# The last projection as seven half-size products instead of eight, with x's sums moved to GpSimd

## The reference, cut to what matters

```python
def conv_ffn(hn, w_up, conv_w, conv_b, w_down):
    u = causal_dwconv(hn @ w_up.astype(hn.dtype), conv_w) + conv_b.astype(hn.dtype)
    a, b = jnp.split(u, 2, axis=-1)
    return (jax.nn.silu(a) * b) @ w_down.astype(hn.dtype)

h = h + conv_ffn(rmsnorm(h, norm2[layer]), ...)   # w_down: 2816 x 1024
h = rmsnorm(h, norm_f)
return h[:, N_META:]
```

## Time and profile before

| What | us |
|---|---|
| runs (median; lowest to highest) | 2037.92; 2035.79 to 2041.82 |
| the profiled execution's own time | 2038.91 |
| its span | 2037.1 |
| PE busy | 1983.4 (97%) |
| DVE busy | 1220.9 (60%) |
| ACT busy | 770.8 (38%) |
| GpSimd busy | 287.2 (14%) |
| DMA queue, share of 16 engines | 43.0% |

### The profile page before, as it was taken

How to read it: one execution, slowest core, us unless ns; L and a number is a source line. 1 busy time by engine, 2 the same in 40 slices (tenths; PEclk the granted TensorE clock), 3 DMA queues, 4 the chain that set the end, 5 groups by cost and what they waited for, 6 DMA issues and landing times.

```text
span 2037.1 us, 31749 instructions
## 1 busy us (share of the span) xinstructions
PE 1983.4 (97%) x13268; PEld 1902.2 (93%) x13268; DVE 1220.9 (60%) x1476; ACT 770.8 (38%) x1022; POOL 287.2 (14%) x276
## 2 busy tenths in 40 slices
PE   8999999999999999999999999997999999999998
PEld 8999998999999999899999999997999999988886
DVE  6457674666577555666533343389888787743533
ACT  5213333534333444434343333244444444332322
POOL 0000003659280122222000001100000000000101
PEclk9999999999999999999999999998999999999999
DMA  9235567664456664555342223311222221274442
GB/s 285 87 108 130 147 164 194 194 197 156 149 148 161 159 180 148 149 156 169 92 183 99 83 91 88 100 60 56 84 73 84 73 90 67 85 282 139 142 144 108
DMA packets 271619, 270.21 MB, mean 133 GB/s; under 512 B 147772, under 2 KB 215716, under 8 KB 271348
## 3 DMA queue, kind: packets, MB, share of 16 engines
q1 hardware_dynamic: 271476, 268.17, 43.0%
HBM read 188.55 MB, written 79.57 MB: 132 GB/s over the span
## 4 chain that ended last, share of the span: by engine, by line
PE 87%; DVE 6%; issue 2%; DMA 2%; ACT 2%; SPq 2%; DVEq 0%; ACTq 0%
PE a_psum L1046 32%; PE a_psum L1349 18%; PE a_psum L1358 12%; PE a_psum L154 10%; PE a_psum L1033 5%; PE a_psum L1121 1%; PE a_psum L1140 1%; PE a_psum L1225 1%; PE a_psum L1150 1%; PE a_psum L1103 1%; PE a_psum L1118 1%; PE a_psum L1166 1%; DMA w_raw<-in_w_in 1%; DVE ext L2097 1%; PE a_psum L1240 1%
## 5 line engine op out<-in xcount | busy, mean ns | idle before, releaser
L1046 PE MATMUL a_psum<-xh,w_hi 128*128 128x342 f32 (+3 forms) x1656 | 536.2, 324 | 1.4 <-DVE w_lo L1789 1.3
L1046 PE MATMUL a_psum<-xl,w_hi 128*128 128x342 f32 (+3 forms) x1656 | 531.9, 321 | 0.0
L1046 PE MATMUL a_psum<-xh,w_lo 128*128 128x342 f32 (+3 forms) x1656 | 530.0, 320 | 0.0
L1046 PEld LDWEIGHTS a_psum<-xh,w_hi 128*128 128x128 f32 x1656 | 312.7, 189 | 4.2 <-DVE w_lo L1789 1.9
L1046 PEld LDWEIGHTS a_psum<-xl,w_hi 128*128 128x128 f32 x1656 | 312.8, 189 | 1.0
L1046 PEld LDWEIGHTS a_psum<-xh,w_lo 128*128 128x128 f32 x1656 | 312.6, 189 | 0.0
L1493 ACT ACTIVATE post<-a_psum 128x342 f32<-128x342 f32 (+3 forms) x207 | 94.4, 456 | 553.3 <-PE a_psum L1046 516.5
L1789 DVE TENSOR_TENSOR w_lo<-w_raw,w_hi 128x1024 fp32r<-128x1024 f32 x87 | 110.2, 1267 | 153.6 <-ACT w_hi L1418 153.6
L1358 PE MATMUL a_psum<-act_hi,down_hi 128*128 128x512 f32 x352 | 139.7, 397 | 3.4 <-DVE act_lo L2298 3.4
L1358 PE MATMUL a_psum<-act_hi,down_lo 128*128 128x512 f32 x352 | 139.7, 397 | 0.0
L1358 PE MATMUL a_psum<-act_lo,down_hi 128*128 128x512 f32 x352 | 139.2, 396 | 0.0
(11 more groups left out here) (272 smaller groups left out, 3921.2 us busy)
## 6 DMA issues: line engine op xcount, KB each, us to landing
w_raw<-in_w_in SPq DMA_DIRECT2D x76, 512.0 KB, 3.8
down_raw<-in_w_ffn_down SPq DMA_DIRECT2D x44, 512.0 KB, 3.6
up_raw<-in_w_up SPq DMA_DIRECT2D x19, 1024.0 KB, 4.9
mix_scratch<-post SPq DMA_DIRECT2D x32, 522.0 KB, 2.8
act_scratch<-post SPq DMA_DIRECT2D x22, 512.0 KB, 2.6
act_raw<-act_scratch SPq DMA_DIRECT2D x44, 256.0 KB, 3.9
ext<-mix_scratch SPq DMA_DIRECT2D x9, 1024.0 KB, 7.0
y<-mix_scratch SPq DMA_DIRECT2D x18, 512.0 KB, 5.8
```

The lines of the kernel that those rows point to most:

```text
L1046: mm = pe.matmul(psum[:, u % 2, 0:n], w[:, k, :], x[:, k, at0:at0 + n], start=(k == 0 and part == 0), stop=(k == KC - 1 and part == 2))
```

## The change

1. The down projection becomes a 2x2 block product made of seven products: 11 k-tiles of 128 (KH) against 4 tiles of 128 output channels and 512 tokens, 77 steps of 4 x 3 matmuls. Each step loads a 128x512 weight tile and a 128x512 activation tile. With p the product, operands are blocks of w_down and of the activation, or sums of blocks.
2. The sums of w_down (`ws`, four) are made in DRAM by eight transfers on GpSimd's own queue: four copies at input tile 5, two accumulating transfers at tile 12, and one each at tiles 77 and 80. Each is 1408 x 512 floats.
3. The sums of the activation (`ts`, four) are made by GpSimd as each block's product is done (`act_sums`): one 128x512 instruction for j under 11, three for j from 11 on; SP stores them (`store_sums`), and for j from 11 on first loads the partner block's half and sum (`load_sums`). ACT's first taps wait for these.
4. The results of the seven products are added on DVE (`down_add`, eight instructions of 128x2048, and eight of 128x256 at the end), with one ACT copy out of PSUM (128x2048).
5. Eight weight slots instead of six; three steps are prepared ahead of the seam (DEARLY) where it was one, the fourth between the last block's taps, and the rest behind `store_sums(21)` on SP. The ACT table for Ln and Exp is loaded at the seam, not at the end.
6. The last four steps run in two chunks of 256 tokens; the norm runs over three column ranges, with 24 output transfers.
7. At the change of form, x's four sums, the first pair's four quarter sums and the split of x block 5 go from DVE to GpSimd; the first pair's products come in the order 0, 2, 3, 1, 4, 5, 6; one `x_low` waits for the last sum.

```diff
-NDOWN = 2 * FT
-DW, DA, DIN = 6, 8, 3
+KH = FT // 2
+NDOWN = 7 * KH
+DW, DA, DIN, DEARLY = 8, 8, 3, 3
...
+            def load_sums(j):
+                k = j - KH
+                sp.wait_ge(act_st[k % 2], 16 * (k // 2 + 1))
+                sp.wait_ge(sum_st, sums_stored(j - 1))
+                sp.dma_start(ts_one[:, :], sc["act"][k][:, 512:1024]).then_inc(sum_in, 16)
+                sp.dma_start(ts_two[:, :], sc["ts"][0, k]).then_inc(sum_in, 16)
+            def store_sums(j):
+                for n, (kind, x) in enumerate(((0, ts_one),) if j < KH else
+                                              ((2, ts_one), (1, ts_two), (3, acc_of(j, 1)[:, 0:512]))):
+                    sp.wait_ge(p_q, summed_act(j) if j < KH else summed_act(j - 1) + n + 1)
+                    sp.dma_start(sc["ts"][kind, j % KH], x[:, 0:512]).then_inc(sum_st, 16)
...
+                store_act(j - 1)
+                store_sums(j - 1)
+                if j >= KH:
+                    load_sums(j)
...
+            def down_operands(q):
+                p, k = q // KH, q % KH
+                w = io["w_ffn_down"][0]
+                first, second = w[k * P:k * P + P, :], w[(KH + k) * P:(KH + k) * P + P, :]
+                into_w = (first[:, 0:512], sc["ws"][1, k], second[:, 0:512], sc["ws"][0, k], sc["ws"][2, k], sc["ws"][3, k],
+                          second[:, 512:1024])[p]
+                into_a = (sc["act"][k][:, 0:512], sc["ts"][1, k], sc["act"][KH + k][:, 0:512], sc["ts"][0, k],
+                          sc["ts"][2, k], sc["act"][KH + k][:, 512:1024], sc["ts"][3, k])[p]
+                return into_w, into_a
...
             def load_down(q):
-                half, kb = q // FT, q % FT
+                p, k = q // KH, q % KH
+                if q == KH:
+                    sp.wait_ge(w_sums, 128)
...
+            for q in range(DEARLY + 1):
+                load_down(q)
             store_act(FT - 1)
-            for q in range(2, NDOWN):
+            store_sums(FT - 1)
+            for q in range(DEARLY + 1, NDOWN):
                 load_down(q)
-                if q == 5:
-                    sp.dma_start(res[:, :, 2 * H2 - SEQ:2 * H2], sc["hres"].rearrange("m p t -> p m t")).then_inc(h_in, 16)
-            for half in range(2):
+                if q % 3 == 1 and q < 3 * KC + 4:
+                    m = (q // 3 + 3) % KC
+                    sp.dma_start(res[:, m, 2 * H2 - SEQ:2 * H2], sc["hres"][m]).then_inc(h_in, 16)
...
+                for n in product_order(i):
                     if i == 0:
-                        pe.wait_ge(x2_split, part_of(n))
+                        pe.wait_ge(*low_of(n))
...
+            def down_step(q, m, c0=0, n=512):
+                p, k = q // KH, q % KH
                 w, x = q % DW, q % DA
-                for part, (a, b) in enumerate(((dw_high[w], da_high[x]), (dw_high[w], da_low[x]), (dw_low[w], da_high[x]))):
-                    mm = pe.matmul(psum[:, m, :], a[:, m * P:m * P + P], b[:, :], start=(kb == 0 and part == 0),
-                                   stop=(kb == FT - 1 and part == 2))
-                if kb == FT - 1:
-                    mm.then_inc(d_bank, 1)
-                elif last:
-                    mm.then_inc(d_used, 1)
...
+                hi, lo = (y[w][:, m * P:m * P + P] for y in (dw_high, dw_low))
+                for part, (a, b) in enumerate(((hi, da_high[x]), (hi, da_low[x]), (lo, da_high[x]))):
+                    mm = pe.matmul(psum[:, (0, 4, 0, 4, 0, 4, 0)[p] + m, c0:c0 + n], a, b[:, c0:c0 + n],
+                                   start=(p not in (2, 5, 6) and k == 0 and part == 0),
+                                   stop=(k == KH - 1 and part == 2), skip_group_check=(p in (2, 5, 6)))
+                return mm
...
+            for ch in range(2):
+                for m in range(4):
+                    if ch:
+                        pe.wait_ge(added, C12_DONE + m + 1)
+                    for q in range(NDOWN - TAIL, NDOWN):
+                        mm = down_step(q, m, 256 * ch, 256)
+                    mm.then_inc(d_bank, 1)
+                    if ch == 1 and m == 1:
+                        left_sums(0)
+            left_sums(1)
...
+                    for q in range(DEARLY):
+                        down_high(q)
                 first_tap(j, 0)
             first_tap(FT - 1, 1)
             gate_silu(FT - 1)
-            for q in range(1, FT + 6):
+            table(LNEXP)
...
+            for q in range(DEARLY, NDOWN):
+                if q == KH + 4:
+                    act.wait_ge(d_bank, 1)
+                    act.activation(d_one[:, :, :], psum[:, 0:4, :], ACT.Copy).then_inc(c11, 1)
                 down_high(q)
...
-            def x_sums(n):
-                if n == 0:
-                    dve.wait_ge(x_prep, KC + 1)
-                    dve.tensor_tensor(t1[:, :, :], b11, b12, ALU.subtract).then_inc(x_prep, 1)
...
-                    x_sums(2)
-                    for n in range(4):
-                        quarter_sum(0, n)
                     x_part_low(0)
                     for n in range(4):
+                        quarter_split(0, n)
...
+            for n in LOWS[1:5]:
+                x_part_low(n)
+            taps(J0 - 1, 1)
             combine(0, 0)
-            x_part_low(4)
             combine(0, 1)
-            taps(J0 - 1, 0)
-            x_part_low(5)
+            combine(0, 2)
             x_part_low(6)
-            taps(J0 - 1, 1)
             gate_product(J0 - 1)
...
+            down_low(DEARLY)
             taps(FT - 1, 1)
             gate_product(FT - 1)
...
+            def down_add(n):
+                c11_, c12_, c21_, c22_ = quad(0, 0), quad(0, 1), quad(1, 0), quad(1, 1)
+                low, high = psum[:, 0:4, :], psum[:, 4:8, :]
+                dve.wait_ge(d_bank, (2, 2, 2, 2, 3, 4, 5, 6)[n])
+                if n == 0:
+                    dve.wait_ge(c11, 2 * NPAIR + 1)
+                    ins = dve.tensor_tensor(d_two[:, :, :], high, d_one[:, :, :], ALU.subtract)
+                elif n < 4:
+                    dve.wait_ge(h_in, 32 + 16 * KC)
+                    dve.wait_ge(added, U_MADE)
+                    c = (c22_, c12_, c21_)[n - 1]
+                    ins = dve.tensor_tensor(c, c, d_two[:, :, :], ALU.subtract if n == 2 else ALU.add)
+                else:
+                    c, of, op = ((c11_, low, ALU.add), (c22_, high, ALU.subtract), (c22_, low, ALU.subtract),
+                                 (c12_, high, ALU.add))[n - 4]
+                    dve.wait_ge(added, U_USED if n < 6 else n)
+                    ins = dve.tensor_tensor(c, c, of, op)
+                ins.then_inc(added, 1)
...
+                if kind == "proj" and a == (5, 0):
+                    pool.wait_ge(units_done, tiles_done(4))
+                    for into, of in zip(ws, (a21, a11, a11, a12)):
+                        pool.dma_start(into, of).then_inc(w_sums, 16)
+                elif kind == "proj" and a == (12, 0):
+                    pool.wait_ge(units_done, tiles_done(11))
+                    pool.wait_ge(w_sums, 64)
+                    pool.dma_start(ws[0], a22, accum_op=ALU.add, max_dma_last_dim=4 * 512).then_inc(w_sums, 16)
+                    pool.dma_start(ws[2], a21, accum_op=ALU.add, max_dma_last_dim=4 * 512).then_inc(w_sums, 16)
...
+                    pool.dma_start(ws[3], ws[1], accum_op=ALU.add, max_dma_last_dim=4 * 512).then_inc(w_sums, 16)
...
+            def x_sums(n):
+                if n == 0:
+                    pool.wait_ge(x_prep, KC + 1)
+                    pool.tensor_tensor(t1[:, :, :], b11, b12, ALU.subtract).then_inc(x_prep, 1)
...
+            def first_quarter_sums():
+                raw_, sums = u_raw[0], u_sum[0]
+                a11, a12, a21, a22 = raw_[:, 0, 0:4, :], raw_[:, 0, 4:8, :], raw_[:, 1, 0:4, :], raw_[:, 1, 4:8, :]
+                pool.wait_ge(*pair_in(0))
+                for n, of in enumerate(((a21, a22), (a11, sums[:, 0, :, :]), (a11, a21), (a12, sums[:, 1, :, :]))):
+                    if n in (1, 3):
+                        pool.wait_ge(w_sum, 1 if n == 1 else 2)
+                    pool.tensor_tensor(sums[:, n, :, :], *of, ALU.add).then_inc(w_sum, 1)
+            def act_sums(j):
+                a0, left, right = acc_of(j, 0), slice(0, 512), slice(512, 1024)
+                pool.wait_ge(prod, j + 1)
+                if j < KH:
+                    if j:
+                        pool.wait_ge(sum_st, sums_stored(j - 1))
+                    pool.tensor_tensor(ts_one[:, :], a0[:, left], a0[:, right], ALU.subtract).then_inc(p_q, 1)
+                else:
+                    pool.wait_ge(sum_in, 16 * (NCH + 2 * (j - KH + 1)))
+                    pool.tensor_tensor(ts_one[:, :], a0[:, right], ts_one[:, :], ALU.subtract).then_inc(p_q, 1)
+                    pool.tensor_tensor(ts_two[:, :], ts_two[:, :], a0[:, right], ALU.add).then_inc(p_q, 1)
+                    pool.wait_ge(p_q, summed_act(j - 1) + 2)
```

(12 more changed lines are left out.)

366 lines of the change are left out of this document (194 added, 172 removed).

## The result

| | median (lowest to highest), us | ratio to before, 95% interval |
|---|---|---|
| before | 2038.39 (2035.79 to 2041.82), 14 runs | 1 |
| changed | 2044.42 (2041.73 to 2050.53), 14 runs | 1.003 [1.0023, 1.0037] |

A forecast was written before the change was run, and what follows sets the result against it. PE's matmuls were taken to bound the pair and down stages. 2038.9 - 29.7 (matmuls) - 2.2 (end) + 3.4 (change of form) + 13.0 (seam) + 0.6 (clock) = 2024.0, so 2023 us against the median; range 2009 to 2034.

The forecast's parts named there:

- The transfers for w_down's sums: Eight DRAM transfers, most in the first stage: cost 0, allowance 3 us, an estimated 9 us each.
- The seam: Pairs to down stage: late loads behind SP's stores make PE idle 16.4 us, before 3.4; +13.0, bounds +3.5 and +16.
- The change of form: Before pair 1: DVE and GpSimd take turns, PE waits 9.4 us for a split of x; +3.4, bounds -12 and +7.
- The matmuls: Down stage: fewer PE matmuls, 216.2 us against 245.9; -29.7, bounds -30 and -19.
- The clock: PE's granted clock falls after waits; one more such stretch costs +0.6 us, bounds 0 and 3.
- The end: After the last product: SP's queue of output transfers takes 9.8 us, before 12.0; -2.2, bounds -4 and 0.
- The pairs slip: Rival in the pairs: GpSimd's three sums make PE wait 1 us in 11 pairs; 2034 us, chance 0.09.
- the loads bind: Rival in the down stage: landings of 7.5 us make steps 3.2 us, +26; 2049 us, chance 0.06.
- No turns: Rival at the change of form: DVE and GpSimd needn't take turns, so it gains 12 us; 2007.6 us, chance 0.12.
- The side "slower": Outcome for the whole kernel: the changed kernel is slower than before, chance 0.06.

The follow-up runs named there:

- x1: Changed kernel without the eight transfers for w_down's sums, down steps reading same-size w_down blocks instead: 2023.36 us, ratio 0.9918.
- x3: Kernel before plus only the eight transfers, at tiles 5, 12, 77 and 80, their results unread: 2059.26 us, ratio 1.0091.
- x5: Changed kernel, transfers in place, with the weight loads of tiles 15 to 17 issued on ACT's queue instead of SP's: 2038.60 us, ratio 1.0.
- x2: Changed kernel with the same eight transfers moved into the pairs, about 20 us apart: 2023.71 us, ratio 0.9919.
- x12: x2 with only SP's order at the seam changed, loads of down steps ahead of the last blocks' stores: 2007.81 us, ratio 0.9849.
- x7: x2 with x's sums, the first pair's quarter sums and the split of x block 5 back on DVE, in the old order: 2023.10 us, ratio 0.9932.
- x8: x2 with GpSimd's eight sums at the change of form replaced by memsets of the same tiles: 2013.36 us, ratio 0.988.
- x6: x2 with SP's loads ahead of stores at the seam and ACT's and DVE's orders there changed too: 2002.04 us, ratio 0.9824.
- x10: Changed kernel with the four copies at tile 12 instead of 5 and the two accumulating transfers at tile 68: 2048.96 us, ratio 1.005.
- x4: Changed kernel with only the two accumulating transfers moved from tile 12 to tile 68: 2024.60 us, ratio 0.9924.

## Why the prediction was wrong

**The transfers for w_down's sums: this step failed.** I priced them at 0 with an allowance of 3; they cost 19 to 23 us (x1, x3). The argument was that no wait after 1200 us is for a transfer and that the earlier stage loads its weights a tile ahead. The first was no evidence on the stage in which six of the eight run. The second was about the load's lead, and not about SP's queue: the stage issues 16 stores of 128-byte pieces between two loads, and these are what a large transfer beside them draws out, 34.6 us for 10.7. The load behind them went out 24.6 us late, PE waited 17.9 us, and DVE's next transposes waited for the same stores (x5). I gave this no rival, though the sentence "No row shows a transfer issued by GpSimd" stood in it: the cost of something that no row shows had no upper end worked out. The figure of the Trainium skill (DMA: Bandwidth & Descriptors, Anatomy of one DMA) priced the transfers alone (an estimated 9 us each); part 6 of after's profile says otherwise for this mix:

```profile
down_sums<-in_w_ffn_down POOLq DMA_DIRECT2D x6, 2816.0 KB, 30.2
```

In x2, one by one, the same six landed in 13.6 by the median, still over 9.

**The seam: right.** Forecast 16.4 us of waits with the longest 12.6, measured 16.3 and 12.0, by the forecast's chain; x12 shows that SP's order made 12.6 of the 15.7 that x2 waits.

**The change of form: right in kind and nearly in size, its cause only in part.** 9.6 us for 9.4 forecast on the same split, 1.5 and 2.3 on others as forecast; the taps' 14.7 us are the turns. GpSimd's x sums took 4.7 to 5.6 us instead of 4.5, and its split 7.9. The stretch with the pairs grew by 3.0 for 3.4. The prediction put this down to x's sums and three activation sums together; by x7 the move of x's sums has 0.9 of it. With memsets, the stretch was 6.5 us shorter than before (x8, 554.3), where the rival without turns said 12.

**The matmuls: right, somewhat more.** The down stage without waits and at full clock took 214.5 (x6) for 216.2 forecast. In the earlier trace rows 434 matmuls went into 100 us; now it is 440, without a change to the instruction. The windows from 1850 us, before and after:

```profile
1850.00:1950.00 100.00, 100.00 (x436) 81.63 (x435) 43.09 (x44) 34.27 (x46) 6.46 (x5) 1.00 0.43 142
```
```profile
1850.00:1950.00 100.00, 100.00 (x440) 82.18 (x439) 64.67 (x84) 47.43 (x80) 4.79 (x3) 1.00 0.67 216
```

Why one is 1% closer together stays open; no run was made for it.

**The clock: undersized.** +0.6 was forecast. At the seam 4.9 us were lost behind 15.7 us of waits (x2 against x6), where before lost about 2.6 by the prediction's count, half of it in the window of the earlier trace rows, so +2.3. In x2 the level fell behind the first wait (0.66 from 1780 to 1785 us) and behind the last. The 1.7 us that the matmuls took less than forecast cancel this: that x1 and x2 landed within 1 us of 2023 is in part luck. Some 2 more are part of the front stage's 22.6: behind its wait PE made 29 matmuls in 6.4 us, where 42 would go at the rate of 65 in 10.

```profile
200.00:210.00 10.00, 6.43 (x29) 6.43 (x30) 4.27 (x6) 3.43 (x5) 0.00 (x0) 0.62 0.74 210
```

**The end: right in kind, 0.6 short.** 9.8 was forecast, 10.4 came, by SP's queue of output transfers as I took it. The chain that ended last closes with DVE's `finish`, until 2040.5, but the timeline shows SP behind by then: it issues one transfer after another, 0.49 us apart, and is done at 2042.1, 1.6 us after DVE.

```profile
2037.73 2.74 DVE residual_T L2412 x7
```
```profile
2034.29 7.83 SPq L1085 DMA_DIRECT2D out<-residual_T  x16
```

**The rivals.** "The pairs slip" and "the loads bind" didn't happen: PE is fully busy with 833 matmuls in 100 us of the pairs (from 1500) and 440 in 100 of the down steps. "No turns" is refuted by the taps and by x7. The side "slower" was right to keep, at 0.06, but for a mechanism that I had not named.

## What to carry to other kernels

A transfer that "fits in the idle bandwidth" has to be placed against what the issuing queues do at that moment, not against an average DMA share: look for bursts of stores in small pieces, and at who stands behind them on the queue and on the engine that refills their buffers. The same eight transfers cost some 20 us with two of them at tile 12, and nothing with all eight in the pairs. And at a seam between two stages, loads whose data have long been there should stand on the queue ahead of stores that wait for the last product. Work moved from DVE to GpSimd is no gain by itself when both read SBUF: what DVE saves it can lose in turns (x7).

## What the runs showed of the hardware

- SP is held at the issue of a store in 128-byte pieces while large transfers of another queue run: up to 12.0 us for one that takes 0.56 alone (x10), and about in proportion to the number beside it (against x4, 22.6 us of delay for two accumulating transfers, 11.3 for one; 24.7 for four copies). A 512 KB weight load issued beside them landed in at most 12.3 us (x10), where 4.0 is usual there. The Trainium skill (DMA: Bandwidth & Descriptors, Queues, rings and completion order) says that each DMA engine serves its queues in turn, a packet at a time. By that rule a queue of small pieces would lose most against one of large pieces. The trace agrees with it, but no run here varies the piece, so the cause is argued and not shown. That the engines were simply full isn't excluded either: the share was 1.08 to 1.24 there, and 0.93 from 1500 to 1600 us in x2, where PE didn't wait.
- DVE's two-input instructions keep their 5.11 us for four taps beside GpSimd memsets (x8); beside GpSimd sums they took 14.70.
- The down stage's matmuls came 1% closer together after the change (440 in 100 us for 436), for no reason that a run shows.
